# A feed-forward stage in which 9 of 22 gate/up pairs are computed as seven block products for eight, and the down product in two parts

## The chip, the cores and the metric

One core of a Trainium2 chip (trn2), one launch. The metric is device time in microseconds (us), the median of three runs. Engines are named as in the profile: PE is TensorE's matmuls, PEld its weight loads, DVE is VectorE, ACT is ScalarE, POOL is GpSimd, SP is the engine that issues the weight transfers.

## The reference, cut to what matters

x holds 512 tokens of 1024 channels. Two blocks of one kind and one of another run one after the other; each has a token mixer (not touched here), and together they have four feed-forward stages of this form, with 2816 = 22 x 128 inner channels:

```
h = rms_norm(x, w_norm)
g = h @ w_gate            # 1024 -> 2816
u = h @ w_up              # 1024 -> 2816
x = x + s * ((silu(g) * u) @ w_down)   # 2816 -> 1024, s is 1.0 or 0.5
```

All of it is float32. After the last stage comes a final rms_norm.

## The kernel before, in words

**Layout.** Channels lie on the 128 partitions and tokens along the free dimension, so x is 8 tiles of 128x512. A product is made of rows: one 128x128 block of weights times one 128x512 tile. Each operand is split into a rounded high part and the rest (WHI, WLO for the weights; HHI, HLO for h; FHI, FLO for the inner activations), and a row is three matmuls, lines 1469 to 1471: high x high, high x rest of the tile, rest of the weights x high. One output tile of gate or up is 8 rows (24 matmuls of 512 columns).

**A feed-forward stage** (`ffn`, line 505). For each j of 22: the gate product, then on DVE `gs` (line 2278: PSUM times the root of the norm), on ACT `silu` (line 1873), the up product, on DVE `mul` (line 2285), on ACT `fhi` (line 1877, the high part), on DVE `flo` (line 2289, the rest). Then the down product: 8 output tiles of 22 rows each, and for each tile `add` on DVE (lines 2299 and 2301). The norm's scale is applied after the product, which is why h itself is only x times a weight. The last tile of the last stage is computed in two halves of 256 tokens (`last_tile`, line 531; matmuls on lines 1558 to 1560), and each half goes through `hadd` (lines 2313, 2314), the final norm's sums and root, and eight `hscale` (line 2324) before it is stored. `last_half` (line 553) emits hadd, hsq, hsum, hroot and the eight hscale of a half.

**Weights.** They come as one stream of slots, each up to 8 rows (512 KB). SP loads slot k into one of four raw buffers (`load`, line 2730; it waits for the split of slot k - 4). ACT casts the high part (`high`, line 1805), DVE subtracts it (`low`, line 2216). Four split buffers: `high` of slot k waits until PE has finished slot k - 4.

**The order of work.** `Order` (line 209) simulates the whole kernel and emits one list of steps; every engine runs its steps in that list's order, and waits on semaphores. PE's steps advance the planner's clock `now`; a step of another engine gets an end time from that engine's own backlog and the table `TIMES`, and the planner does not make it wait for steps it depends on. A *chain* (a generator) sleeps until a time or until the end time of a step, and is resumed at the next `beat`, which comes after each PE row. `advance` (line 270) emits `high` for slots up to three past the last one taken and less than four past the last one released; `split` emits the slot's `low` once `high` has its end time. These few lines set how the splits are ordered:

```
while self.next_split < min(self.next_slot + look, self.used + SPL, len(self.slots)):
    self.spawn(self.split(k, self.add("high", k)))
...
for engine, us in TIMES.get(step[0], ()):
    t = self.engine_end[engine] = max(t, self.engine_end[engine]) + us
```

Entries of TIMES used below (us): row 0.68, high 1.0031, low 1.23, gs 1.005, silu 1.4753, mul 0.64242, fhi 1.0912, flo 0.21674; HANDOVER, added to each end time, is 0.17528. The change adds srow 0.36, snap 0.4, dd 0.45, ww 1.0, cc 0.95, tsum 3.0, thi 1.03, tlo 1.23, padd 2.5532. They are the planner's figures, not measurements.

## Time and profile before

| | us |
|---|---|
| median of 3 runs | 2700.85 (2699.92 to 2701.69) |
| span of the profiled execution | 2697.8 |
| PE busy in it | 2665.9 (99%) |
| PEld busy | 2195.1 (81%) |
| DVE busy | 1526.9 (57%) |
| ACT busy | 1173.5 (43%) |

The span runs from the first to the last instruction of one execution. Its own device time was not listed apart from the runs; the median lies 3.05 us above the span. A matmul's duration in the trace includes its way through the array, so consecutive matmuls overlap, and what a stream costs is read from the distance of their starts. "idle before <- X" names what ended an engine's wait.

### The profile page before, as it was taken

How to read it: one execution, taken by the hardware profiler on the slowest of the kernel's cores; microseconds unless marked ns; L12 is line 12 of the kernel's file. 1: busy time of each engine (PE TensorE's matmuls, PEld its weight loads, DVE VectorE, ACT ScalarE, POOL GpSimd, SP SyncE). 2: the span in 40 equal slices, each digit the busy share in tenths (PEclk: the TensorE clock that was granted, in tenths of full speed). 3: DMA queues.
4: the chain of work that ended last, by engine and by line, in shares of the span. 5: the costliest groups of instructions: out<-in, count | busy, mean ns of one | idle time of the engine just before them, and what ended most of it. 6: DMA issues, size and time to landing. Idle time of an engine off the chain costs nothing.

```text
span 2697.8 us, 33846 instructions
## 1 busy us (share of the span) xinstructions
PE 2665.9 (99%) x13860; PEld 2195.1 (81%) x13860; DVE 1526.9 (57%) x2142; ACT 1173.5 (43%) x1732; POOL 26.8 (1%) x45
## 2 busy tenths in 40 slices
PE   9989999999989999999999999999999999999998
PEld 8777888888777888888888888888777888888887
DVE  7885444345885444344444356899978844544433
ACT  6784332225784322233322234455688452432221
POOL 0000000000000000000000000000000000000000
PEclk9999999999999999999999999999999999999999
DMA  6303333324303333333333342222223432333332
GB/s 216 94 2 110 100 96 95 98 83 148 94 2 110 102 94 97 97 94 97 100 94 96 98 138 86 72 74 76 77 86 96 133 94 94 98 98 94 98 94 67
DMA packets 75801, 255.55 MB, mean 95 GB/s; under 512 B 9088, under 2 KB 12288, under 8 KB 75264
## 3 DMA queue, kind: packets, MB, share of 16 engines
q1 hardware_dynamic: 73136, 240.29, 29.3%
q0 software_dynamic: 2512, 13.11, 1.3%
q8 instruction: 110, 1.80, 0.3%
q14 instruction: 43, 0.35, 0.0%
HBM read 241.30 MB, written 8.39 MB: 93 GB/s over the span
## 4 chain that ended last, share of the span: by engine, by line
PE 93%; DVE 4%; ACT 3%; issue 1%; DVEq 0%; ACTq 0%
PE PS L1469 27%; PE PS L1471 27%; PE PS L1470 27%; PE PS L1719 1%; PE PS L1701 1%; PE PS L1428 1%; PE PS L1488 1%; PE PS L1487 1%; PE PS L1489 1%; DVE WLO L2216 0%; PE PS L1665 0%; ACT WHI L1805 0%; PE PS L1537 0%; PE PS L1535 0%; PE PS L1539 0%
## 5 line engine op out<-in xcount | busy, mean ns | idle before, releaser
L1469 PE MATMUL PS<-HHI,WHI 128*128 128x512 f32 x2256 | 893.2, 396 | 0.0
L1471 PE MATMUL PS<-HHI,WLO 128*128 128x512 f32 x2256 | 878.8, 390 | 0.0
L1470 PE MATMUL PS<-HLO,WHI 128*128 128x512 f32 x2256 | 878.3, 389 | 0.0
L2216 DVE TENSOR_TENSOR WLO<-WR,WHI 128x1024 fp32r<-128x1024 f32 (+2 forms) x450 | 535.0, 1191 | 495.4 <-ACT WHI L1805 492.2
L1805 ACT CAST WHI<-WR 128x1024 fp32r<-128x1024 f32 (+2 forms) x450 | 457.5, 1018 | 445.6 <-PE PS L1471 421.9
L1469 PEld LDWEIGHTS PS<-HHI,WHI 128*128 128x128 f32 x2256 | 423.6, 188 | 92.1 <-issue 4.8
L1470 PEld LDWEIGHTS PS<-HLO,WHI 128*128 128x128 f32 x2256 | 423.7, 188 | 89.9 <-issue 4.1
L1471 PEld LDWEIGHTS PS<-HHI,WLO 128*128 128x128 f32 x2256 | 423.4, 188 | 88.8
L1469 PE MATMUL PS<-FHI,WHI 128*128 128x512 f32 x682 | 265.3, 389 | 0.0
L1470 PE MATMUL PS<-FLO,WHI 128*128 128x512 f32 x682 | 265.3, 389 | 0.0
L1471 PE MATMUL PS<-FHI,WLO 128*128 128x512 f32 x682 | 265.3, 389 | 0.0
L1877 ACT CAST FHI<-SQF 128x512 fp32r<-128x512 f32 x88 | 54.5, 620 | 330.3 <-DVE SQF L2285 330.3
L1873 ACT ACTIVATE SQF<-SQF 128x512 f32<-128x512 f32 x88 | 55.6, 632 | 307.4 <-DVE SQF L2278 307.3
L2606 DVE SCALAR_TENSOR_TENSOR CVA<-CU,VEC,CVA 128x511 f32<-128x511 f32 (+14 forms) x240 | 162.9, 730 | 1.8 <-ACT CVA L2110 1.8
L2285 DVE TENSOR_TENSOR SQF<-SQF,PS 128x512 f32<-128x512 f32 x88 | 60.6, 688 | 166.0 <-PE PS L1471 162.1
L1469 PEld LDWEIGHTS PS<-FHI,WHI 128*128 128x128 f32 x682 | 128.0, 188 | 26.8
L1470 PEld LDWEIGHTS PS<-FLO,WHI 128*128 128x128 f32 x682 | 128.0, 188 | 26.5
L1471 PEld LDWEIGHTS PS<-FHI,WLO 128*128 128x128 f32 x682 | 128.0, 188 | 26.4
L2278 DVE TENSOR_TENSOR SQF<-PS,RS 128x512 f32<-128x512 f32 x88 | 60.8, 691 | 142.2 <-PE PS L1471 140.9
L1469 PE MATMUL PS<-YHI,WHI 128*128 128x512 f32 x320 | 128.1, 400 | 2.2 <-DVE WLO L2216 2.1
L1471 PE MATMUL PS<-YHI,WLO 128*128 128x512 f32 x320 | 124.7, 390 | 0.0
L1470 PE MATMUL PS<-YLO,WHI 128*128 128x512 f32 x320 | 124.6, 389 | 0.0
(381 smaller groups left out, 2727.5 us busy)
## 6 DMA issues: line engine op xcount, KB each, us to landing
WR<-in_stream SPq DMA_DIRECT2D x402, 512.0 KB, 3.6
WR<-in_stream SPq DMA_DIRECT2D x32, 384.0 KB, 3.0
xkeep<-X POOLq DMA_DIRECT2D x3, 2048.0 KB, 9.4
X<-xkeep POOLq DMA_DIRECT2D x24, 256.0 KB, 4.7
WR<-in_stream SPq DMA_DIRECT2D x16, 328.0 KB, 4.0
ROT<-RQ SPq DMA_DIRECT2D x40, 64.0 KB, 2.0
X<-in_xin SPq DMA_DIRECT2D x8, 256.0 KB, 4.9
out<-X SPq DMA_DIRECT2D x8, 256.0 KB, 2.2
```

Source lines behind the costliest of these rows:

```text
L1428: t = e.transpose(out[:, i * P:(i + 1) * P], src, ident)
L1469: e.matmul(out, hi[:, i, :], xhi, start=first, stop=False)
L1470: e.matmul(out, hi[:, i, :], xlo, start=False, stop=False)
L1471: t = e.matmul(out, lo[:, i, :], xhi, start=False, stop=final)
L1487: e.matmul(out, xhi, hi[:, i, :], start=r == 0, stop=False)
L1805: e.copy(hi, raw).then_inc(S["act_high"], 1)
L1873: e.activation(SQ[:, j % 2, :], SQ[:, j % 2, :], ACT.Silu).then_inc(S["act_silu"], 1)
L1877: e.copy(FHI[:, j, :], HF[:, j % 2, :]).then_inc(S["act_xhigh"], 1)
L2216: e.tensor_tensor(lo, raw, hi.bitcast(F32), ALU.subtract).then_inc(S["dve_low"], 1)
L2278: e.tensor_tensor(SQ[:, j % 2, :], PS[o.bank["gate", f, j]][:, :], RS[:, :], ALU.mult).then_inc(S["dve_gs"], 1)
L2285: e.tensor_tensor(HF[:, j % 2, :], SQ[:, j % 2, :], PS[o.bank["up", f, j]][:, :], ALU.mult).then_inc(S["dve_mul"], 1)
L2606: e.scalar_tensor_tensor(acc[:, s:T], CU[:, j, 0:T - s], vec("cvw", 8 * (TAPS - 1 - s) + j), acc[:, s:T], ALU.mult, ALU.add).then_inc(S["d ...
```

## The change

Of the 22 gate/up pairs of each stage, the nine with j = 5, 7, ..., 21 (`SEVEN`) are computed in another way. The block matrix [gate, up] (two halves of 512 input channels each) times the two halves of 256 tokens is a 2x2 by 2x2 block product, and it is formed by seven products (Strassen's scheme in Winograd's form) in place of eight. One product is 4 rows of three matmuls with 256 columns. At the start of a stage `combined` makes four sums of the tokens' blocks (`sv`, `ss`, `sd`, split by `sshi`, `sslo`). For each such pair `weight_sums` makes four sums of the weight blocks on DVE (`tsum`, four adds of 512 columns from the two raw slots), splits them (`thi` on ACT and `tlo` on DVE, two of 1024 columns each), and during and after the products DVE and ACT put the outputs together (`snap`, `dd`, `ww`, a `gs` in two halves, `cc`). The up slot's own split covers half of its columns. The sums' buffers also serve for the outputs, so `tsum` of pair j waits for `mul` of pair j - 2.

The down product is in two parts of 11 rows (`PARTS`): after pair 10 all eight output tiles get their first 11 rows and are added to x (`padd`), after pair 21 the other 11. FHI and FLO shrink to 11 tiles each. A down tile's weights come in slots of 6 and 5 rows. In a stage the planner gives six PSUM banks to the products and two to the rest, before four and four.

The diff, cut; `eight` is the loop body of before:

```diff
...
 SPL = 4
 LOOK = 3
 SLOT = 1024
+PARTS = (range(0, 11), range(11, 22))
+PART = 11
+DOWN = (((0, 6), (6, 5)), ((11, 6), (17, 5)))
+SEVEN = range(5, FT, 2)
+PRODUCTS = ((0, 0, True), (1, 0, True), (2, 0, True), (0, 1, False), (0, 0, False), (1, 0, False), (2, 0, False))
 HALVES = (slice(0, T // 2), slice(T // 2, T))
 LEVELS = (1, 2, 4, 8, 16, 32, 64)
...
             fm("w_in", l, c * P)
         for j in range(DT):
             fm("w_out", l, j * P)
-        for j in range(FT):
-            fm("w_gate", l, j * P)
-            fm("w_up", l, j * P)
-        for j in range(DT):
-            fm("w_down", l, j * P, down)
+        for part, down in zip(PARTS, DOWN):
+            for j in part:
+                fm("w_gate", l, j * P)
+                fm("w_up", l, j * P)
+            for j in range(DT):
+                fm("w_down", l, j * P, down)
 
...
     def advance(self, look=LOOK):
         while self.next_split < min(self.next_slot + look, self.used + SPL, len(self.slots)):
             k = self.next_split
+            if k - RAW in self.pair_of and not self.summed(self.pair_of[k - RAW]):
+                break
             self.next_split += 1
             self.spawn(self.split(k, self.add("high", k)))
...
+        for pair in SEVEN:
+            at_ = self.slots.index((gate, i, 0, DT, pair * P, P))
+            self.pair_of[at_] = self.pair_of[at_ + 1] = (f, pair)
...
+        self.ring.update(main=(0, 1, 2, 3, 4, 5), side=(6, 7))
+        self.spawn(self.combined(f))
+        for part, rows in zip(PARTS, DOWN):
+            for j in part:
+                if j + 1 in SEVEN:
+                    self.spawn(self.weight_sums(f, j + 1))
+                if j in SEVEN:
+                    self.seven(f, gate, up, i, up0, j)
+                else:
+                    self.eight(f, gate, up, i, up0, j)
+                self.add("fhi", f, j)
+                self.add("flo", f, j)
...
+            if part is PARTS[-1]:
+                self.ring.update(main=(0, 1, 2, 3), side=(4, 5, 6, 7))
+            for j in range(DT):
+                if part is not PARTS[-1]:
+                    self.product(("part", f, j), ("F", f), down, i, j * P, rows)
+                    self.x["padd", f, j] = self.x_now[j]
+                    self.x_now[j] = self.add("padd", f, j)
+                    self.free(("part", f, j), ("dve_add", self.x_now[j]))
+                elif (f, j) == (len(NORM_FFN) - 1, DT - 1):
+                    self.last_tile(f, down, i, j)
+                else:
+                    self.product(("out", ADD_FFN[f], j), ("F", f), down, i, j * P, rows)
+                    self.add_to_x(ADD_FFN[f], AFTER_NORM[m], j)
...
+    def seven(self, f, gate, up, i, up0, j):
+
+        keys = ("seven", f, j, 0), ("seven", f, j, 1), ("seven", f, j, 2)
+        for key in keys:
+            self.take(key)
+        slots = self.slot(gate, i, 0, j * P), self.slot(up, i, 0, up0 + j * P)
+        self.slot_of["seven", f, j] = slots
+        self.run(lambda: ("tlo", f, j, 1) in self.n)
+        for u in range(7):
+            for r in range(4):
+                self.add("srow", f, j, u, r)
+                if r == 3:
+                    if u in (4, 6):
+                        self.release()
+                    else:
+                        self.products += 1
+                        self.product_end[f, j, u] = self.products
+                self.beat()
+            if u == 0 or u == 2:
+                self.add("snap", f, j, u // 2)
+            elif u == 1:
+                self.add("dd", f, j)
+            elif u == 5:
+                self.add("ww", f, j)
+                self.free(keys[0], ("dve_gs", self.add("gs", f, j)))
+                self.add("silu", f, j)
+        self.free(keys[1], ("dve_gs", ("gs", f, j)))
+        self.free(keys[2], ("dve_gs", self.add("cc", f, j)))
...
+
+        yield from self.added(("sslo", f, 3))
+        last = max(k for k, pair in self.pair_of.items() if pair == (f, j))
+        while last - RAW not in self.low:
+            yield 0.1
+        yield self.add("tsum", f, j)
+        self.advance()
+        for k in range(2):
+            self.add("thi", f, j, k)
+        for k in range(2):
+            yield ("thi", f, j, k)
+            self.add("tlo", f, j, k)
 
     def last_tile(self, f, down, i, j):
 
...
+            return hi[:, 4:8, :], lo[:, 4:8, :]
+        i = {1: 1, 2: 0, 3: 3, 5: 2}[u]
+        return (x[:, i, :].rearrange("p (r c) -> p r c", r=4) for x in (THI, TLO))
+
+    def block_tokens(u, r):
+
+        if u in (0, 4):
+            return HHI[:, u + r, HALVES[0]], HLO[:, u + r, HALVES[0]]
+        if u == 3:
+            return HHI[:, 4 + r, HALVES[1]], HLO[:, 4 + r, HALVES[1]]
+        i = {1: 1, 2: 0, 5: 3, 6: 2}[u]
+        return SHI[:, i, r, :], SLO[:, i, r, :]
+
     def totals(j, h):
 
         if h == 1:
...
                     t.then_inc(S["pe_slot"], 1)
+            elif kind == "srow":
+                f, j, u, r = a
+                bank, half, fresh = PRODUCTS[u]
+                k_gate, k_up = o.slot_of["seven", f, j]
...
+                    if fresh:
+                        emptied(q, ("seven", f, j, bank))
+                    if u == 0:
+                        weights_split(q, k_gate)
+                        q.wait_ge(S["dve_ulo"], n["ulo", NORM_FFN[f], DT - 1])
+                    elif u == 1:
+                        q.wait_ge(S["dve_xlow"], n["tlo", f, j, 1])
+                        q.wait_ge(S["dve_xlow"], n["sslo", f, 3])
+                    elif u == 3:
+                        q.wait_ge(S["act_uhi"], n["snap", f, j, 0])
+                    elif u == 5:
+                        q.wait_ge(S["dve_gs"], n["dd", f, j])
+                    elif u == 6:
+                        weights_split(q, k_up)
+                        q.wait_ge(S["act_uhi"], n["snap", f, j, 1])
+                hi, lo = block_weights(f, j, u)
...
                     q.wait_ge(S["pe_slot"], k - SPL + 1)
+                if k in o.pair_of and k - 1 in o.pair_of:
+                    hi, raw = hi[:, T:2 * T], raw[:, T:2 * T]
...
+                if k == 3:
+                    for r in range(4):
+                        t = e.activation(SUMS[3][:, r, :], SV[:, r, :], ACT.Copy, scale=norm_weight(NORM_FFN[f], r))
+                    settle(t)
+                e.copy(SHI[:, k, :, :].rearrange("p r t -> p (r t)"), combination(f, k)).then_inc(S["act_xhigh"], 1)
+            elif kind == "thi":
+                f, j, k = a
+                q.wait_ge(S["dve_scale"], n["tsum", f, j])
+                if j - 2 in SEVEN:
+                    q.wait_ge(S["pe_slot"], o.slot_of["seven", f, j - 2][1] + 1)
+                e.copy(THI[:, 2 * k:2 * k + 2, :].rearrange("p u c -> p (u c)"), WT[k][:, :, :].rearrange("p u c -> p (u c)")
+                       ).then_inc(S["act_xhigh"], 1)
+            elif kind == "snap":
+                f, j, k = a
+                q.wait_ge(S["dve_xlow"], n["tlo", f, j, 1])
+                q.wait_ge(S["pe_prod"], o.product_end[f, j, 2 * k])
+                e.copy((P1, Q5)[k], PS[o.bank["seven", f, j, 2 * k]][:, HALVES[0]]).then_inc(S["act_uhi"], 1)
             elif kind == "uhi":
                 m, j = a
                 x_ready(q, o.x[step])
...
+            elif kind == "tsum":
+                f, j = a
+                k_gate, k_up = o.slot_of["seven", f, j]
+                (gate, _, _), (up, _, _) = slot_tiles(k_gate), slot_tiles(k_up)
+                for k in (k_gate, k_up):
+                    q.wait_ge(s_w[k % RAW], 16 * (k // RAW + 1))
+                if j - 2 in SEVEN:
+                    q.wait_ge(S["dve_mul"], n["mul", f, j - 2])
+                else:
+                    q.wait_ge(S["dve_xlow"], n["sslo", f, 3])
+                settle(e.tensor_tensor(WT[0][:, 0, :], gate[:, 0:T], up[:, 0:T], ALU.add))
+                e.tensor_tensor(WT[1][:, 0, :], up[:, 0:T], up[:, T:2 * T], ALU.add)
+                settle(e.tensor_tensor(WT[0][:, 1, :], WT[0][:, 0, :], up[:, T:2 * T], ALU.add))
+                e.tensor_tensor(WT[1][:, 1, :], WT[0][:, 1, :], gate[:, T:2 * T], ALU.add).then_inc(S["dve_scale"], 1)
...
+            elif kind == "dd":
+                f, j = a
+                q.wait_ge(S["act_uhi"], n["snap", f, j, 0])
+                q.wait_ge(S["pe_prod"], o.product_end[f, j, 1])
+                e.tensor_tensor(DD, PS[o.bank["seven", f, j, 1]][:, HALVES[0]], P1, ALU.subtract).then_inc(S["dve_gs"], 1)
+            elif kind == "ww":
+                f, j = a
+                q.wait_ge(S["pe_prod"], o.product_end[f, j, 5])
+                settle(e.tensor_tensor(WW, PS[o.bank["seven", f, j, 1]][:, HALVES[0]], P1, ALU.subtract))
+                if j >= 2:
+                    q.wait_ge(S["dve_mul"], n["mul", f, j - 2])
+                e.tensor_tensor(SQ[:, j % 2, HALVES[1]], PS[o.bank["seven", f, j, 0]][:, HALVES[1]], WW, ALU.subtract
+                                ).then_inc(S["dve_gs"], 1)
+            elif kind == "gs" and a[1] in SEVEN:
+                f, j = a
+                rooted(q, NORM_FFN[f])
+                q.wait_ge(S["pe_slot"], o.slot_of["seven", f, j][0] + 1)
+                e.tensor_tensor(SQ[:, j % 2, HALVES[0]], PS[o.bank["seven", f, j, 0]][:, HALVES[0]], RS[:, HALVES[0]], ALU.mult)
+                q.wait_ge(S["dve_gs"], n["ww", f, j])
+                e.tensor_tensor(SQ[:, j % 2, HALVES[1]], SQ[:, j % 2, HALVES[1]], RS[:, HALVES[1]], ALU.mult).then_inc(S["dve_gs"], 1)
+            elif kind == "cc":
+                f, j = a
+                q.wait_ge(S["act_uhi"], n["snap", f, j, 1])
+                q.wait_ge(S["dve_gs"], n["gs", f, j])
+                e.tensor_tensor(UP2[:, HALVES[1]], WW, Q5, ALU.add)
+                q.wait_ge(S["pe_slot"], o.slot_of["seven", f, j][1] + 1)
+                e.tensor_tensor(UP2[:, HALVES[0]], PS[o.bank["seven", f, j, 2]][:, HALVES[0]], DD, ALU.add).then_inc(S["dve_gs"], 1)
+            elif kind == "mul" and a[1] in SEVEN:
+                f, j = a
+                q.wait_ge(S["act_silu"], n["silu", f, j])
+                q.wait_ge(S["dve_gs"], n["cc", f, j])
+                q.wait_ge(S["act_xhigh"], n["fhi", f, j - 2])
+                e.tensor_tensor(HF[:, j % 2, :], SQ[:, j % 2, :], UP2, ALU.mult).then_inc(S["dve_mul"], 1)
+            elif kind == "padd":
+                f, j = a
+                done(q, ("part", f, j))
+                x_ready(q, o.x[step])
+                rooted(q, NORM_FFN[f])
+                q.wait_ge(S["dve_add"], n[step] - 1)
+                settle(e.tensor_tensor(HF[:, 0, :], PS[o.bank["part", f, j]][:, :], RS[:, :], ALU.mult))
+                e.scalar_tensor_tensor(X[:, j, :], HF[:, 0, :], ADD_SCALE[ADD_FFN[f]], X[:, j, :], ALU.mult, ALU.add
+                                       ).then_inc(S["dve_add"], 1)
...
                     q.wait_ge(S["dve_low"], n[o.low[k - RAW]])
+                    if k - RAW in o.pair_of:
+                        q.wait_ge(S["dve_scale"], n[("tsum", *o.pair_of[k - RAW])])
...
```

## Rows read from the trace of the kernel before

**Rows 1.** The page, parts 1 and 2: span, busy time and the granted clock
```profile
span 2697.8 us, 33846 instructions
...
PE 2665.9 (99%) x13860; PEld 2195.1 (81%) x13860; DVE 1526.9 (57%) x2142; ACT 1173.5 (43%) x1732; POOL 26.8 (1%) x45
...
PEclk9999999999999999999999999999999999999999
```

**Rows 2.** Windows in the last feed-forward stage: pairs, down product, halved tile
```profile
core 0: us, PE busy (x) PEld busy (x) DVE busy (x) ACT busy (x) POOL busy (x), PEclk, DMA share, GB/s
2352.00:2560.00 208.00, 208.00 (x919) 172.26 (x918) 87.05 (x96) 59.77 (x76) 0.00 (x0) 1.00 0.32 96
...
2572.00:2671.00 99.00, 99.00 (x438) 81.97 (x438) 34.42 (x37) 22.64 (x26) 0.00 (x0) 1.00 0.26 82
2671.00:2688.00 17.00, 17.00 (x137) 16.72 (x136) 5.39 (x12) 3.23 (x5) 0.00 (x0) 1.00 0.04 13
```

**Rows 3.** Timeline, DVE over one pair: start, duration, engine, line, tiles
```profile
2414.80 0.69 DVE L2285 TENSOR_TENSOR SQF<-SQF,PS 128x512 f32<-128x512 f32 x1 [1.95 <-PE PS L1471]
2416.17 0.69 DVE L2289 TENSOR_TENSOR FLO<-SQF,FHI 128x512 fp32r<-128x512 f32 x1 [0.69 <-ACT FHI L1877]
2417.13 1.23 DVE L2216 TENSOR_TENSOR WLO<-WR,WHI 128x1024 fp32r<-128x1024 f32 x1 [0.26 <-ACT WHI L1805]
2420.17 0.69 DVE L2278 TENSOR_TENSOR SQF<-PS,RS 128x512 f32<-128x512 f32 x1 [1.82 <-PE PS L1471]
2425.68 0.69 DVE L2285 TENSOR_TENSOR SQF<-SQF,PS 128x512 f32<-128x512 f32 x1 [1.95 <-PE PS L1471]
```

**Rows 4.** Timeline, ACT over the same pair
```profile
2415.52 0.62 ACT L1877 CAST FHI<-SQF 128x512 fp32r<-128x512 f32 x1 [3.93 <-DVE SQF L2285]
2416.05 1.05 ACT L1805 CAST WHI<-WR 128x1024 fp32r<-128x1024 f32 x1
2420.89 0.63 ACT L1873 ACTIVATE SQF<-SQF 128x512 f32<-128x512 f32 x1 [3.80 <-DVE SQF L2278]
2421.43 1.04 ACT L1805 CAST WHI<-WR 128x1024 fp32r<-128x1024 f32 x1
```

**Rows 5.** Timeline, PE: last 512-column, first and two later 256-column matmuls
```profile
2671.34 0.39 PE L1471 MATMUL PS<-FHI,WLO 128*128 128x512 f32 x1
2671.57 0.28 PE L1558 MATMUL PS<-FHI,WHI 128*128 128x256 f32 x1
...
2679.98 0.28 PE L1558 MATMUL PS<-FHI,WHI 128*128 128x256 f32 x1
...
2683.58 0.28 PE L1558 MATMUL PS<-FHI,WHI 128*128 128x256 f32 x1
```

**Rows 6.** Timeline, DVE, the last tile and the end
```profile
2671.77 0.69 DVE L2299 TENSOR_TENSOR SQF<-PS,RS 128x512 f32<-128x512 f32 x1 [2.20 <-PE PS L1471]
...
2680.54 0.42 DVE L2313 TENSOR_TENSOR SQF<-PS,RS 128x256 f32<-128x256 f32 x1 [5.96 <-PE PS L1560]
2681.00 0.43 DVE L2314 SCALAR_TENSOR_TENSOR X<-SQF,X 128x256 f32<-128x256 f32 x1
2685.54 3.26 DVE L2324 SCALAR_TENSOR_TENSOR X<-X,VEC,SQF 128x256 f32<-128x256 f32 x8 [4.11 <-ACT SQF L1788]
2688.88 0.42 DVE L2313 TENSOR_TENSOR SQF<-PS,RS 128x256 f32<-128x256 f32 x1
```

**Rows 7.** Timeline, a weight split that PE waited for (out-projection of block one)
```profile
230.20 3.50 DVE L2216 TENSOR_TENSOR WLO<-WR,WHI 128x1024 fp32r<-128x1024 f32 x3 [12.62 <-ACT WHI L1805]
...
230.68 0.39 PE L1471 MATMUL PS<-YHI,WLO 128*128 128x512 f32 x1
...
231.48 0.50 PE L1469 MATMUL PS<-YHI,WHI 128*128 128x512 f32 x1 [0.41 <-DVE WLO L2216]
...
231.82 0.40 PE L1470 MATMUL PS<-YLO,WHI 128*128 128x512 f32 x1
```

**Rows 8.** The page, part 6: the weight transfers, KB each, median us to landing
```profile
WR<-in_stream SPq DMA_DIRECT2D x402, 512.0 KB, 3.6
```

More of the change, by code:

```diff
@@ L43 @@
     **dict.fromkeys(["xT", "bT", "zT", "pT"], "turn"),
-    **dict.fromkeys(["add", "hadd"], "add"),
+    **dict.fromkeys(["add", "hadd", "padd"], "add"),
+    **dict.fromkeys(["uhi", "snap"], "uhi"),
+    **dict.fromkeys(["gs", "dd", "ww", "cc"], "gs"),
+    **dict.fromkeys(["scale", "ss", "sd", "tsum"], "scale"),
     **dict.fromkeys(["xscale", "hscale"], "xscale"),
@@ L65, in tm @@
             s.append((name, i, r0, 2, c0, 512))
-    down = ((0, 8), (8, 8), (16, 6))
     for l in range(2):
@@ L353, in product @@
         self.rhs[p] = rhs
+        self.first[p] = rows[0][0]
         self.take(p)
@@ L510, in ffn @@
         self.run()
-        for j in range(FT):
-            if j > 0:
-                self.product(("gate", f, j), ("U", m), gate, i, j * P)
-            self.free(("gate", f, j), ("dve_gs", self.add("gs", f, j)))
-            self.add("silu", f, j)
-            if j > 0:
-                self.product(("up", f, j), ("U", m), up, i, up0 + j * P)
-            self.free(("up", f, j), ("dve_mul", self.add("mul", f, j)))
-            self.add("fhi", f, j)
-            self.add("flo", f, j)
-            if m == 5 and 4 <= j < 4 + DT:
-                self.x["xscale", 4, j - 4] = self.x_now[j - 4]
-                self.x_now[j - 4] = self.add("xscale", 4, j - 4)
@@ L524, in ffn @@
-        for j in range(DT):
-            if (f, j) == (len(NORM_FFN) - 1, DT - 1):
-                self.last_tile(f, down, i, j)
-                continue
-            self.product(("out", ADD_FFN[f], j), ("F", f), down, i, j * P, ((0, 8), (8, 8), (16, 6)))
-            self.add_to_x(ADD_FFN[f], AFTER_NORM[m], j)
+        self.ring.update(main=(0, 1, 2, 3, 4, 5), side=(6, 7))
+        self.spawn(self.combined(f))
+        for part, rows in zip(PARTS, DOWN):
+            for j in part:
+                if j + 1 in SEVEN:
[6 more added lines that the diff above has]
+                self.add("flo", f, j)
+                if m == 5 and 5 <= j < 5 + DT // 2:
+                    self.run(lambda: ("sd", f) in self.n)
+                    for t in (2 * j - 10, 2 * j - 9):
+                        self.x["xscale", 4, t] = self.x_now[t]
+                        self.x_now[t] = self.add("xscale", 4, t)
+            if part is PARTS[-1]:
+                self.ring.update(main=(0, 1, 2, 3), side=(4, 5, 6, 7))
+            for j in range(DT):
+                if part is not PARTS[-1]:
[8 more added lines that the diff above has]
+                    self.add_to_x(ADD_FFN[f], AFTER_NORM[m], j)
@@ new lines, in eight @@
+    def eight(self, f, gate, up, i, up0, j):
+        m = NORM_FFN[f]
+        if j > 0:
+            self.product(("gate", f, j), ("U", m), gate, i, j * P)
+        self.free(("gate", f, j), ("dve_gs", self.add("gs", f, j)))
+        self.add("silu", f, j)
+        if j > 0:
+            self.product(("up", f, j), ("U", m), up, i, up0 + j * P)
+        self.free(("up", f, j), ("dve_mul", self.add("mul", f, j)))
+    def seven(self, f, gate, up, i, up0, j):
[22 more added lines that the diff above has]
+                self.free(keys[0], ("dve_gs", self.add("gs", f, j)))
+                self.add("silu", f, j)
+        self.free(keys[1], ("dve_gs", ("gs", f, j)))
+        self.free(keys[2], ("dve_gs", self.add("cc", f, j)))
+        self.add("mul", f, j)
@@ L544, in last_tile @@
         self.spawn(self.last_half(0))
-        for r in range(FT):
+        for r in PARTS[-1]:
             _, i, nr = self.slot_of[p, r]
@@ L1411, in x_ready @@
         kind, i, *j = made if made[0] != "xload" else (made[0], 0, made[1])
-        if kind == "xload":
+        if kind == "padd":
+            q.wait_ge(S["dve_add"], n[made])
+        elif kind == "xload":
             q.wait_ge(s_x[j[0]], 16)
@@ L1473, in tensor_engine @@
                     t.then_inc(S["pe_slot"], 1)
+            elif kind == "srow":
+                f, j, u, r = a
+                bank, half, fresh = PRODUCTS[u]
+                k_gate, k_up = o.slot_of["seven", f, j]
+                out = PS[o.bank["seven", f, j, bank]][:, HALVES[half]]
+                if r == 0:
+                    if fresh:
[14 more added lines that the diff above has]
+                hi, lo = block_weights(f, j, u)
+                xhi, xlo = block_tokens(u, r)
+                kw = {"skip_group_check": True}
+                e.matmul(out, hi[:, r, :], xhi, start=fresh and r == 0, stop=False, **kw)
+                e.matmul(out, hi[:, r, :], xlo, start=False, stop=False, **kw)
+                t = e.matmul(out, lo[:, r, :], xhi, start=False, stop=r == 3, **kw)
+                if r == 3:
+                    t.then_inc(S["pe_slot" if u in (4, 6) else "pe_prod"], 1)
             elif kind == "trow":
```

128 lines of the change are left out of this document (105 added, 23 removed).

## The prediction

> **What bounds the kernel now.** I read the page first, then windows by stage, then the timeline of one pair engine by engine. On the page PE is busy for 99% of the span and its granted clock stands at the upper level, 2.4 GHz, in every slice [rows 1]; in the windows of a feed-forward stage PE is busy for all of each window, at pairs, down product and halved tile alike, with DVE at 42% and ACT at 29% in the pairs [rows 2]. So PE's stream sets the time, and DVE's and ACT's work costs nothing as long as it arrives in time. What a stream costs is the distance of starts. Two `mul` lie 10.88 us apart [rows 3], 48 matmuls of 512 columns, 0.2267 each. From 2679.98 to 2683.58 there are 30 steps of 256 columns, 0.1200 each [rows 5], at the same clock [rows 2].
>
> **What it removes on PE.** A pair of seven products is 84 matmuls of 256 columns, 84 x 0.1200 = 10.08, for 10.88: 0.80 less. Nine pairs, four stages: 36 x 0.80 = **-28.8 us**. Both widths carry 0.0133 above their columns at 2.4 GHz (0.2133 and 0.1067), and with 1.75 times the matmuls this eats 36 x 36 x 0.0133 = 17 us of the ideal gain of 46. The down product keeps its rows, 8 x 22, so its PE time is unchanged.
> The Trainium skill (TensorE: Matmul & The Clock Gate, Back-to-back issue gap) has a gap of N/2.4 + 2.5 ns, 215.8 and 109.2 ns for these widths; by it a pair would fall from 10.36 to 9.17 us and the gain would be 43 us. The rows differ from it, and the sum goes by them.
>
> **The end: +4.0.** In the last tile the second half's rows run on PE while the first half is normalised. Its `hadd` starts at 2688.88, just behind the eight `hscale` of the first half (2685.54 + 3.26 = 2688.80) [rows 6]. The list order stays (the planner emits the first half's eight `hscale` at its last row of half two, before the second `hadd`), so all behind the first half keeps its times, but PE has 11 rows to do there instead of 22: 11 x 3 x 0.1200 = 4.0 us of PE work moves ahead of it and is no longer hidden.
>
> **Smaller parts, at nothing.** `padd` is 2 x 0.69 on DVE per down tile, which lasts 7.5 us; two slots of 6 and 5 rows cost one split more per 15 us; the cover is DVE's idle half. Without it a down tile would wait for a bank, and there are six. The token sums are 12 operations of 256 columns, one of 1024 and four splits of 1.23: about 11 us of DVE and 7.5 of ACT, over pairs 1 to 4 (43 us), where DVE's own work is 2 x 1.23 + 3 x 0.69 = 4.5 us a pair [rows 3]. `tsum` of pair 11 waits on DVE for a transfer (3.6 us to landing [rows 8]) in the down product's sixth tile; the next split in its queue is wanted 10 us later. In pairs SP's load of slot k waits for `tsum` too; it has some 10 us in hand.
>
> **The sums of the weights: the term that decides.** A block-product pair (call its start 0) is followed by an ordinary one (10.08) and the next block-product pair (20.96), whose second product needs the second `tlo` at 22.40. `tsum` needs the buffers that `mul` of the pair before frees. I follow the planner's list through one such period. At the end of the fifth product (7.20) the gate slot is released and `high`, `low` of the next gate are emitted; the planner has `low` due at 8.38 and emits it at the beat of 8.64, ahead of `ww`. After pair and `mul`, `flo`, it emits `tsum` at the first beat of the ordinary pair, to end at 16.86. That is after 15.52, where `gs`, `silu` of the ordinary pair and `high` of the next slot are emitted. So the orders are: DVE low, ww, gs, cc, mul, flo, tsum, low, gs, low, tlo, tlo; ACT high, silu, fhi, high, silu, high, thi, thi.
> Durations: 256 columns 0.42 [rows 6]; 512 columns 0.69, 1024 columns 1.23 [rows 3]; ACT 0.62 and 1.04 [rows 4]. An operation behind an independent one starts 0.09 before that one's end [rows 4, 7], behind a dependent one on its engine 0.04 after [rows 6], behind another engine 0.03 after [rows 3, 4], behind PE's boundary 0.20 after [rows 5, 6]. (ACT's wait there I take as 0.25.)
> - high 7.45 to 8.49, low to 9.75; ww 9.66 to 10.54, gs to 11.20, cc 11.24 to 11.99 (PE ended the pair at 10.08, so DVE is late by then);
> - mul to 12.72, fhi to 13.37, flo 13.40 to 14.09, tsum (four adds, two settled) to 16.75, half low to 17.35, gs to 17.95;
> - silu to 18.61, high 18.52 to 19.56, low 19.59 to 20.82 (DVE idle 1.6 us behind that cast), tlo to 21.96, tlo to 23.10.
> Wanted at 22.40: 0.70 late. PE resumes with a loss: in the trace a split ended at 230.20 + 1.23 = 231.43, and the second matmul started at 231.82, 0.39 later for 0.23 [rows 7], so +0.16: **0.86 us a pair**. Everything here hangs on PE's clock of the pair, so the wait comes again each period and doesn't fade. It concerns pairs 7, 9, 13, 15, 17, 19, 21, which have such a pair two before: 28 in all, 28 x 0.86 = **+24.1 us**. In the third stage two `xscale` follow `flo` of pairs 5 and 7 (2 x 0.60 = 1.2 each time, a 512-column operation at 0.69 less the overlap): **+2.4**.
> Below, the wait could be 0.45 (twenty operations, 0.02 less each), above 1.4 (0.03 more each, for the semaphore waits that no row of before shows between halves): 13 to 39 us. I take 0.86, as every duration in it has a row. Steps added behind the late `tlo`: `mul` to 23.7, fhi to 24.35, high to 25.3, `snap` (a 256-column copy, taken as 0.42) to 25.65; PE wants it before the fourth product, at 23.26 + 2.88 = 26.15. It holds by 0.5.
> **Sum:** -28.8 + 4.0 + 24.1 + 2.4 = +1.7. Other stages are replanned from a slightly other state: +-3, at 0. The span would be 2699.5, and with the 3.05 between span and median 2702.6. I allow one more microsecond for a first wait where a stage's DVE queue is late, and say **2704**.
>
> **Rivals.**
> 1. *The sums arrive in time.* For it: DVE work per period is about 16 of 20.96 us, and 0.70 is 3% of the chain; if the true list puts `thi` ahead of `silu` and `high` of the ordinary pair, the cast's 1.04 and the idle 1.6 go. Against: the order follows from the table with 1.3 us to spare. Then -28.8 + 4.0 and up to 2.4: 2676 to 2679. Chance 0.25.
> 2. *A second wait behind the first* (the other side). `snap` of the first product has 0.5 us in hand on ACT, and `mul`, `fhi` and a cast must pass first, all behind the late `tlo`. If these four handovers take 0.5 us more than reckoned, PE stops again ahead of the fourth product, and everything behind the fifth product moves with it. From there each further 0.5 to 1.0 a pair is 14 to 28 us: 2718 to 2732. For it: the queue is in order on both engines. Against: every handover of before takes 0.03 [rows 3, 4]. Chance 0.12.
> 3. *The 256-column stream is not 0.1200 in this place.* It was measured on 66 rows of one kind. At 0.124: 36 x 84 x 0.004 = +12, 2716; chance 0.05. With a fixed part of 2.5 ns rather than 13.3 both widths would be faster, the gain 43 and the end 2690; the trace shows neither width at it, chance 0.01. The Trainium skill's gap (the same section) is that case; the trace disagrees with 13.3.
> 4. The change does what it says on PE (84 matmuls for 48 stand in the code), so that rival has no chance of its own.
>
> **How the numbers follow.** The forecast case has 0.57: 0.86 within 0.45 to 1.4, and +-3 elsewhere, gives 2688 to 2721. The range takes in rival 1 down to 2676 and the foot of rival 2 up to 2724, and leaves out some 0.12. A measurement of this kernel tells about 0.2% from no change, 5.4 us: 2695.4 to 2706.3. Of the forecast case 0.15 falls below that, 0.48 inside, 0.37 above. Faster: 0.25 + 0.01 + 0.09 = 0.35. Same: 0.27. Slower: 0.21 + 0.12 + 0.05 = 0.38. The forecast's middle lies in "same", but no case of size does.
>
> **What would show it.** Right: 256-column matmuls 0.1200 apart in the new lines; in the list of waits, PE waiting for the DVE split of the weight sums 28 times, 0.7 to 0.9 us each, and in no other place of these stages; DVE's `low` ahead of `ww`; PE's busy share under 99%; the first half's `hscale` still ending 8.5 us after that half. Wrong: no such wait (rival 1), a wait of PE for ACT's copy of the first product (rival 2), other spacing (rival 3), or idle PE at the starts of stages or in the down products, which I costed at nothing.

## The result and the profile after

The changed kernel takes **2716.78 us** (median of 4 runs, 2715.88 to 2718.63), the kernel before beside it 2700.39 (4 runs): ratio 1.0062, 95% interval 1.0048 to 1.0077. That is 16 us slower. The forecast was 2704 in a range of 2676 to 2724, so the sign it leaned to and the range held, and the size was 13 us short. The profiled execution has a span of 2714.1 us, against 2697.8 [rows 1].

A line of the page of the changed kernel, part 1:

```profile
PE 2647.5 (98%) x15123; PEld 2235.5 (82%) x15123; DVE 1823.8 (67%) x2738; ACT 1380.4 (51%) x2028; POOL 26.7 (1%) x45
```

PE is down from 99% to 98%, with 84 matmuls of 256 columns in place of 48 of 512 in each of 36 pairs. The list of waits of PE in the changed kernel (us in total, times, longest):

```profile
PE PS L1634 <- DVE TLO L2459: 30.0, 29, 5.8
PE PS L1733 <- ACT SQF L2054: 5.2, 1, 5.2
```

The first line is new: PE waits for the split of the weight sums (`tlo`), 29 times. The second, PE's last sum behind the second half's square, stood before too, at 1.4 us. In the timeline of PE in the changed kernel (two regular waits, one period apart):

```profile
478.33 0.28 PE L1636 MATMUL PS<-HHI,WLO 128*128 128x256 f32 x1
479.42 0.35 PE L1634 MATMUL PS<-SHI,THI 128*128 128x256 f32 x1 [0.82 <-DVE TLO L2459]
479.62 0.28 PE L1635 MATMUL PS<-SLO,THI 128*128 128x256 f32 x1
...
479.85 0.28 PE L1634 MATMUL PS<-SHI,THI 128*128 128x256 f32 x1
...
480.20 0.28 PE L1634 MATMUL PS<-SHI,THI 128*128 128x256 f32 x1
...
501.43 0.36 PE L1634 MATMUL PS<-SHI,THI 128*128 128x256 f32 x1 [0.81 <-DVE TLO L2459]
```

Once it runs, the stream goes at 0.36 per three, as [rows 5] have it. The two waits are 22.01 us apart, where the prediction's period is 20.96: 1.05 is lost. By the starts: the matmul was due at 478.45 and started at 479.42, 0.97 late, and the next came 0.20 behind it instead of 0.12. (The 0.82 shown as idle begins at the modelled end of the matmul before, 0.28 behind its start.)

The timeline of DVE in the changed kernel, from the `flo` of one block-product pair to the late `tlo` (x2 is both halves):

```profile
491.60 0.69 DVE L2576 TENSOR_TENSOR FLO<-SQF,FHI 128x512 fp32r<-128x512 f32 x1 [0.69 <-ACT FHI L2075]
492.21 0.68 DVE L2452 TENSOR_TENSOR WT<-WR 128x512 f32<-128x512 f32 x1
...
495.46 0.68 DVE L2565 TENSOR_TENSOR SQF<-PS,RS 128x512 f32<-128x512 f32 x1
497.79 1.23 DVE L2416 TENSOR_TENSOR WLO<-WR,WHI 128x1024 fp32r<-128x1024 f32 x1 [1.64 <-ACT WHI L1972]
498.93 2.35 DVE L2459 TENSOR_TENSOR TLO<-WT,THI 128x1024 fp32r<-128x1024 f32 x2
```

This is the order of the prediction, with the idle 1.64 us behind the cast of the next slot (1.6 there). The period's zero, reckoned back from its sixth product (start 485.24, less 7.20), is 478.04, so the second `tlo` ends at 501.28 = 23.24, where the prediction had 23.10 and PE wants it at 22.40.

**One wait is unlike the others.** The timeline of PE and then windows of the changed kernel, pair 5 of the third stage (columns of windows: length; busy us and instructions of PE, PEld, DVE, ACT, POOL; granted clock):

```profile
1278.24 0.28 PE L1636 MATMUL PS<-HHI,WLO 128*128 128x256 f32 x1
1284.32 0.55 PE L1634 MATMUL PS<-SHI,THI 128*128 128x256 f32 x1 [5.80 <-DVE TLO L2459]
...
1285.10 0.41 PE L1634 MATMUL PS<-SHI,THI 128*128 128x256 f32 x1
1285.32 0.41 PE L1635 MATMUL PS<-SLO,THI 128*128 128x256 f32 x1
```

```profile
1280.00:1290.00 10.00, 5.68 (x37) 5.71 (x38) 6.34 (x7) 6.03 (x8) 0.00 (x0) 0.66 0.47 168
1290.00:1300.00 10.00, 10.00 (x63) 9.01 (x62) 6.30 (x12) 4.11 (x5) 0.00 (x0) 1.00 0.03 12
```

PE stood 5.8 us, and when it went on, the granted clock was at the lower level for some 3 us: starts 0.215 apart instead of 0.120 (1285.10, 1285.32), about 1.4 us more. The timeline of DVE there in the changed kernel says why the sums are late: the last split of the token sums ends only at 1274.96, just ahead of `tsum` and 2.0 us ahead of pair 5's start on PE (1276.93). In the first stage it ends 9.3 us ahead of it (299.55 for 308.87).

```profile
1273.74 1.22 DVE L2440 TENSOR_TENSOR SLO<-SUM,SHI 128x1024 fp32r<-128x1024 f32 x1
1275.10 0.69 DVE L2452 TENSOR_TENSOR WT<-WR 128x512 f32<-128x512 f32 x1
...
1281.82 2.35 DVE L2459 TENSOR_TENSOR TLO<-WT,THI 128x1024 fp32r<-128x1024 f32 x2
```

**Where the 16.3 us of span come from** (starts in the two traces, a stage being from its first `gs` to the last addition into X): stages 1, 2 and 4 come out even, within 0.2 us (for stage 4 its end is taken apart), so their 7.2 us of gain each are paid back by their waits; stage 3 is longer by 9.8; the end by 3.85; the stretch between stages 1 and 2 by 1.2 and that between 3 and 4 by 1.7. That is 16.5, and the small rests take 0.2 off.

The last two can be read in the traces. The 1.2 is one wait of PE that the kernel before has not, in the mixer between the first and second stages (0.9 idle, the rest in the restart):

```profile
PE PS L1605 <- ACT Z L2083: 0.9, 1, 0.9
```

The 1.7 is the granted clock. In the mixer between the third and fourth stages PE stops for 1.89 us in both kernels. The timeline of PE at the stop and the window behind it, first of the kernel before, then of the changed one:

```profile
2060.46 1.98 PE L1766 MATMUL PS<-XB,GW 128*128 128x512 f32 x4 [1.89 <-DVE XB L2613]
2062.00:2066.00 4.00, 4.00 (x19) 3.11 (x18) 3.85 (x6) 3.97 (x5) 0.00 (x0) 1.00 0.49 136
```

```profile
2071.34 2.88 PE L1931 MATMUL PS<-XB,GW 128*128 128x512 f32 x4 [1.89 <-DVE XB L2900]
2072.00:2076.00 4.00, 4.00 (x10) 2.30 (x9) 3.93 (x6) 3.96 (x5) 0.00 (x0) 0.57 0.42 133
```

Behind the same stop the clock stayed up in one execution and fell in the other. That mixer is not touched by the change, and changed kernels without the fall exist too (e5_order2, e11_best7 below), so this 1.7 us is no steady part of the change.

### The profile page after: what moved, and what is told of

Its sections match the earlier page's. It is cut to its first block, busy times and chain, and to the rows that moved or that the text cites. A ratio compares the mean times of both kernels' runs of the same rounds, so it can differ in the third digit from the quotient of the medians.

```text
span 2714.1 us, 37462 instructions
## 1 busy us (share of the span) xinstructions
PE 2647.5 (98%) x15123; PEld 2235.5 (82%) x15123; DVE 1823.8 (67%) x2738; ACT 1380.4 (51%) x2028; POOL 26.7 (1%) x45
## 4 chain that ended last, share of the span: by engine, by line
PE 74%; DVE 17%; ACT 6%; issue 3%; DVEq 0%; ACTq 0%
PE PS L1605 18%; PE PS L1606 18%; PE PS L1607 18%; DVE WLO L2416 4%; PE PS L1634 3%; PE PS L1636 3%; PE PS L1635 3%; ACT WHI L1972 3%; DVE TLO L2459 2%; PE PS L1884 1%; PE PS L1866 1%; PE PS L1564 1%; DVE WT L2453 1%; DVE WT L2452 1%; DVE SQF L2565 1%
## 5 line engine op out<-in xcount | busy, mean ns | idle before, releaser
L2416 DVE TENSOR_TENSOR WLO<-WR,WHI 128x1024 fp32r<-128x1024 f32 (+4 forms) x482 | 518.9, 1081 | 450.3 <-ACT WHI L1972 447.9
L1972 ACT CAST WHI<-WR 128x1024 fp32r<-128x1024 f32 (+4 forms) x482 | 448.3, 931 | 514.1 <-PE PS L1607 410.7
L1605 PE MATMUL PS<-HHI,WHI 128*128 128x512 f32 x1680 | 670.5, 399 | 0.9 <-ACT Z L2083 0.9
L1607 PE MATMUL PS<-HHI,WLO 128*128 128x512 f32 x1680 | 654.9, 390 | 0.0
L1606 PE MATMUL PS<-HLO,WHI 128*128 128x512 f32 x1680 | 654.9, 390 | 0.0
L1605 PEld LDWEIGHTS PS<-HHI,WHI 128*128 128x128 f32 x1680 | 315.8, 188 | 70.6 <-issue 5.0
L1607 PEld LDWEIGHTS PS<-HHI,WLO 128*128 128x128 f32 x1680 | 315.5, 188 | 67.0
L1606 PEld LDWEIGHTS PS<-HLO,WHI 128*128 128x128 f32 x1680 | 316.0, 188 | 66.2 <-issue 4.4
L1634 PE MATMUL PS<-SHI,THI 128*128 128x256 f32 x432 | 125.0, 289 | 30.0 <-DVE TLO L2459 30.0
L1635 PE MATMUL PS<-SLO,THI 128*128 128x256 f32 x432 | 122.7, 284 | 0.0
```

The source lines that it names most:

```text
L1605: e.matmul(out, hi[:, i, :], xhi, start=first, stop=False)
L1606: e.matmul(out, hi[:, i, :], xlo, start=False, stop=False)
L1607: t = e.matmul(out, lo[:, i, :], xhi, start=False, stop=final)
L1634: e.matmul(out, hi[:, r, :], xhi, start=fresh and r == 0, stop=False, **kw)
L1635: e.matmul(out, hi[:, r, :], xlo, start=False, stop=False, **kw)
L1972: e.copy(hi, raw).then_inc(S["act_high"], 1)
```

## The experiments

Each is an edit of the changed kernel. The runs of before beside them had medians of 2699.91 (e1 to e4), 2700.67 (e5 to e8) and 2700.65 us (e9 to e11).

**e1_parts: the change without its block products**

```
-SEVEN = range(5, FT, 2)
+SEVEN = range(0)
-        self.spawn(self.combined(f))
-                    self.run(lambda: ("sd", f) in self.n)
```

> All 22 pairs of a stage as eight products again; the down product stays in two parts, with its smaller slots, padd and six banks. Theory A (the tail): the parts cost only what is no longer hidden at the end, +4.0 us, so 2704 to 2705; PE waits nowhere in the four stages; the first half's hscale end about 9 us after that half, as in the changed kernel. Rival B (the parts themselves stall PE: banks, slots of 6 and 5 rows, padd): well above 2706, with PE's waits inside the down products. Rival C (the parts are free): 2700.4.

2705.39 us, ratio 1.0020 (1.0011 to 1.0029), +5.5 us. The split `tlo` is gone from the waits, the four stages take their old time (within 0.01 us, the end apart), and PE waits in none of their down products: rival B did not occur. So the two-part down product alone costs 5.5. Its trace has 3.85 at the end and 1.2 in the wait for `Z` of above, so theory A missed that wait. The profiled execution took 2707.48 us, 2.1 more than the median, and has two stretches of lower clock, at the mixer's stop of above (1.7 us) and near 186 us (about 1.1). What the 36 block-product pairs add to that is 16.4 - 5.5 = 10.9 us: they lose by themselves.

**e2_order: the weight sums' splits straight behind the sums, in both queues**

```
-        yield self.add("tsum", f, j)
+        self.add("tsum", f, j)
```

> All of the change, but the planner emits the casts of the weight sums (thi) at once behind tsum instead of at tsum's planned end, so that on ACT they stand ahead of silu and the next slot's cast, and on DVE both tlo stand ahead of gs and the next low. PE's list is the same, the work is the same. Theory A (the order of the lists makes the wait): the second tlo is ready some 2 us early, the 27 regular waits of PE (1.06 us each with the restart, 2.4 in the third stage) go, and pair 5 of the third stage waits about 3 us less: 2716.8 less 31 less 3, 2682 to 2687, faster than both kernels. Rival B (DVE as a whole is too full, 67% busy and more in the stages): the wait moves to another place, mul, snap or a weight split, and the time stays above 2700.

2717.26 us, ratio 1.0065 (1.005 to 1.008): nothing gained, against theory A. The wait moved. The waits of this kernel:

```profile
PE PS L1634 <- ACT WT L2001: 25.7, 26, 2.2
...
PE PS L1634 <- DVE TLO L2459: 3.6, 1, 3.6
```

Its timeline, DVE, PE and ACT in turn:

```profile
496.66 2.36 DVE L2459 TENSOR_TENSOR TLO<-WT,THI 128x1024 fp32r<-128x1024 f32 x2 [0.52 <-ACT THI L1995]
498.94 0.68 DVE L2565 TENSOR_TENSOR SQF<-PS,RS 128x512 f32<-128x512 f32 x1
501.25 1.23 DVE L2416 TENSOR_TENSOR WLO<-WR,WHI 128x1024 fp32r<-128x1024 f32 x1 [1.64 <-ACT WHI L1972]
```

```profile
505.00 0.39 PE L1634 MATMUL PS<-HHI,THI 128*128 128x256 f32 x1 [0.92 <-ACT WT L2001]
```

```profile
503.11 0.62 ACT L2075 CAST FHI<-SQF 128x512 fp32r<-128x512 f32 x1 [1.89 <-DVE SQF L2572]
...
504.59 0.36 ACT L2001 COPY WT<-PS 128x256 f32<-128x256 f32 x1
```

`tlo` is early now, but the ordinary pair's `gs` stands behind both of them, and with it `silu`, the cast of the next slot, that slot's split, `mul`, `fhi`, one more cast and only then ACT's copy of the first product. PE stands ahead of the fourth product: the place that the prediction's rival 2 named, at 0.92. The idle 1.64 on DVE is still there, behind `gs` instead of ahead of `tlo`. Both steps are wanted by PE. That the chain through both is too long as long as it holds that idle time is an argument here; the next run tests it.

**e5_order2: `gs` first, then the sums' splits, the cast of the next slot last**

```
         self.free(("gate", f, j), ("dve_gs", self.add("gs", f, j)))
+        ahead = ("tsum", f, j + 1) in self.n and ("thi", f, j + 1, 0) not in self.n
+        if ahead:
+            self.add("thi", f, j + 1, 0)
         self.add("silu", f, j)
+        if ahead:
+            self.add("thi", f, j + 1, 1)
+            self.add("tlo", f, j + 1, 0)
+            self.add("tlo", f, j + 1, 1)
...
-        yield self.add("tsum", f, j)
+        self.add("tsum", f, j)
+        if ("gs", f, j - 1) not in self.n:
+            return
+        yield ("tsum", f, j)
```

> All of the change; in the ordinary pair ahead of a block-product pair the steps are emitted as gs, thi, silu, thi, tlo, tlo, and only then the next slot's cast and low (in the run before, thi stood ahead of gs and silu, and the wait moved to the copy of the first product). Work and PE's list as in the changed kernel. Theory A (the order of two in-order lists makes the wait, not their load): second tlo at 20.8 and the copy of the first product at 24.7, for 22.4 and 25.3 wanted, so no regular wait in stages 1, 2 and 4, at most 0.6 twice in stage 3, and pair 5 of stage 3 waits 2 to 3 us less: 2683 to 2688. Rival B (the two engines can't carry it in any order): a third place waits, about 1 us a pair, and the time stays at 2710 or more.

**2682.76 us**, ratio 0.9939 (0.9922 to 0.9956), 34 us less than the change. Same operations, same data, another order in two queues: the order made the waits, not the load, and rival B is out. Its timeline of DVE and of PE:

```profile
490.56 0.68 DVE L2575 TENSOR_TENSOR SQF<-PS,RS 128x512 f32<-128x512 f32 x1
...
492.89 1.23 DVE L2469 TENSOR_TENSOR TLO<-WT,THI 128x1024 fp32r<-128x1024 f32 x1 [0.50 <-ACT THI L2005]
494.03 1.22 DVE L2426 TENSOR_TENSOR WLO<-WR,WHI 128x1024 fp32r<-128x1024 f32 x1
```

```profile
495.43 0.28 PE L1646 MATMUL PS<-HHI,WLO 128*128 128x256 f32 x1
495.55 0.28 PE L1644 MATMUL PS<-SHI,THI 128*128 128x256 f32 x1
```

The 1.64 us of waiting became work (0.50 is left), the second `tlo` ends at 494.12, and PE takes it at 495.55 with no gap: 1.4 us in hand. In its list of waits one for `tlo` is left, 3.5 us at pair 5 of the third stage (and 0.8 in two for the copy of the first product). In this trace 33 of the 36 block-product pairs take 10.07 us on PE and the period is 20.98, as the prediction had them without waits. At pair 5 of the third stage the wait fell from 5.8 to 3.5; the rest goes with the late token sums (e6_all below emits them early and has no wait there).

**e4_spaced: five of 22 pairs, four apart**

```
-SEVEN = range(5, FT, 2)
+SEVEN = range(5, FT, 4)
...
-                if j - 2 in SEVEN:
+                if j - 4 in SEVEN:
```

> Block products only for pairs 5, 9, 13, 17, 21 (20 of 36 in all), so that no such pair has one two before it and tsum does not wait for a mul that has just been late. Theory A: 20 x 0.80 = -16.0 for PE's stream, the tail +4, the late pair 5 of the third stage +7.5, no regular waits: 2700.4 - 4.5 = 2696, up to 2699 with what the stages between give. Rival B (block products are dear on PE in themselves, spacing or restarts): each pair removed from the changed kernel makes it faster by the same amount, 2716.8 - 16 x 0.45 = 2709.

2698.20 us, ratio 0.9992 (0.9983 to 1.0002). One wait for `tlo` is left, again the 5.8 us at pair 5. In the traces stages 1 and 2 are 3.9 us shorter than before with five such pairs each, 0.78 a pair for the forecast's 0.80: a pair does take about 10.08 us where its sums come in time, and rival B is out. The sum with 20 pairs at 0.80 less, 5.5 for the parts and 7.2 for pair 5 is -3.3, measured -1.7.

**e10_from7: block products from pair 7 on**

```
-SEVEN = range(5, FT, 2)
+SEVEN = range(7, FT, 2)
```

> The changed kernel, with block products from pair 7 on instead of pair 5 (8 pairs a stage, 32 in all). Theory A (pair 5 of the third stage costs its own wait of 5.8 us and 1.4 us of half clock, and pair 7, whose predecessor pair but one is then ordinary, loses its wait too): +3.2 for four block-product pairs less, -7.2, -2.4 (third stage) and -3 x 1.06 for pair 7: -9.6 us, 2706 to 2709. Rival B (the late token sums of the third stage then hold up pair 7 by as much, since DVE's queue is behind for the whole stage): +3.2 - 4 x 1.06, about 2715 to 2717.

2705.46 us, ratio 1.0020 (1.001 to 1.0029); the span fell by 9.8 us (2714.1 to 2704.3), the theory's 9.6, and the median is 0.5 below its range. The third stage alone is 8.8 us shorter. The waits for `tlo` are 24, longest 2.1, so the 5.8 us and pair 7's waits are gone. A window of this kernel where PE had stood:

```profile
1280.00:1290.00 10.00, 10.00 (x45) 8.29 (x45) 5.70 (x7) 3.77 (x6) 0.00 (x0) 1.00 0.30 101
```

No idle time and no lower clock: four gains given up, and the kernel is 11 us faster than the change.

**e3_name: the step `dd` under another name**

```
-    "dd": (("dve", 0.45),)
+    "df": (("dve", 0.45),)
```

The name `dd` also stands in the program's list of steps that need ACT's table of logarithm and exponential, so each block-product pair loads two tables, as the timeline of ACT in the changed kernel has it:

```profile
481.76 1.28 ACT L1963 ACT_TABLE_LOAD   x1
...
485.49 1.05 ACT L1972 CAST WHI<-WR 128x1024 fp32r<-128x1024 f32 x1 [2.06 <-PE PS L1636]
486.56 1.28 ACT L2069 ACT_TABLE_LOAD   x1
489.29 0.63 ACT L2069 ACTIVATE SQF<-SQF 128x512 f32<-128x512 f32 x1 [1.45 <-DVE SQF L2481]
```

> Only the step dd is renamed to df, so that it no longer stands in the table of functions: 72 table loads of 1.28 us on ACT go (two in each block-product pair), nothing else is different. Theory A (they lie in ACT's idle time: the first before the copy of the third product, the second before a silu that waits for gs): 2716 to 2717, no difference. Rival B (they delay silu and with it mul and the sums of the weights): up to 36 x 0.5 = 18 us faster, about 2700.

2717.32 us, ratio 1.0063 (1.0048 to 1.0078): no difference. 72 loads of 1.28 us, 92 us of ACT, lie in time in which ACT waited anyway (1.45 and 2.06 above).

**e8_tail: the first half's eight `hscale` behind the second `hadd`**

```
         self.add("hroot", h)
+        if h == 0:
+            yield from self.added(("hadd", 1))
```

> The changed kernel, only the second half's hadd is emitted ahead of the first half's eight hscale. Theory A (the tail's loss is DVE's queue: the second hadd stands behind 3.3 us of hscale while PE has long been done): PE's last sum no longer waits 5.2 us, the end is 2.5 to 3.5 us earlier, 2713 to 2714.5. Rival (it only swaps which half is late): no difference, 2716 to 2717.

2713.68 us, ratio 1.0049 (1.0034 to 1.0064): 3.1 us less than the change, and PE's last sum waits 1.4 us for 5.2. In the changed kernel the eight `hscale` keep the second `hadd` waiting, in this one `hadd` goes first. First the changed kernel's end, then this one's:

```profile
2701.50 3.26 DVE L2611 SCALAR_TENSOR_TENSOR X<-X,VEC,SQF 128x256 f32<-128x256 f32 x8 [4.96 <-ACT SQF L1953]
2704.67 0.42 DVE L2600 TENSOR_TENSOR SQF<-PS,RS 128x256 f32<-128x256 f32 x1
...
2708.26 3.26 DVE L2611 SCALAR_TENSOR_TENSOR X<-X,VEC,SQF 128x256 f32<-128x256 f32 x8 [2.72 <-ACT SQF L1953]
```

```profile
2703.76 0.42 DVE L2602 TENSOR_TENSOR SQF<-PS,RS 128x256 f32<-128x256 f32 x1 [4.36 <-PE PS L1727]
2704.22 0.43 DVE L2603 SCALAR_TENSOR_TENSOR X<-SQF,X 128x256 f32<-128x256 f32 x1
2704.57 6.42 DVE L2613 SCALAR_TENSOR_TENSOR X<-X,VEC,SQF 128x256 f32<-128x256 f32 x16
```

**e6_all and e9_best: everything together, with and without early token sums.** e6_all is e5_order2, e3_name and e8_tail with the token sums emitted ahead of pair 0, meant for the late sums of the third stage; e9_best is the same without that edit:

```
         self.spawn(self.mean_square(m))
+        self.spawn(self.combined(f))
         self.product_group(("U", m), [(("gate", f, 0), gate, i, 0), (("up", f, 0), up, i, up0)])
         self.run()
         self.ring.update(main=(0, 1, 2, 3, 4, 5), side=(6, 7))
-        self.spawn(self.combined(f))
```

> The run with the new order (gs, thi, silu, thi, tlo, tlo) and three more edits: the four sums of the tokens are emitted during the first pair, ahead of the norm's root; the step dd is renamed, so that 72 table loads on ACT go; the second half's hadd is emitted ahead of the first half's eight hscale. Theory A: pair 5 of stage 3 no longer waits and TensorE keeps its clock there (-4 to -7 against the new order alone), the end is 3 us shorter: 2674 to 2682. Rival (the early sums delay the root, and PE waits for a bank at the third pair): 2683 to 2690.

> The sums of the weights ahead of the up product, the renamed step, and the first half's hscale behind the second hadd; the token sums stay where the change has them (that is the kernel with everything together, less the early token sums). Theory A (early token sums were what made that kernel 15 us slower than the reordered one): 2682.8 less 3.1 for the tail, 2679 to 2681. Rival B (it was the renamed step or the tail together with the new order): 2692 to 2699 again. Rival C (the two gains overlap): 2682 to 2684.

e6_all: 2698.13 us, ratio 0.9991 (0.9982 to 1.0). e9_best: **2680.23**, ratio 0.9926 (0.991 to 0.9943). The early sums cost 18 us. They did remove the wait of pair 5, and put another at each stage's start (theory A of e9_best holds); PE's waits in e6_all, and one of them in its timeline:

```profile
PE PS L1617 <- DVE WLO L2428: 18.2, 8, 5.3
```

```profile
895.01 0.76 PE L1617 MATMUL PS<-HHI,WHI 128*128 128x512 f32 x1 [5.27 <-DVE WLO L2428]
```

Its timeline of DVE ahead of that:

```profile
888.80 1.23 DVE L2452 TENSOR_TENSOR SLO<-SUM,SHI 128x1024 fp32r<-128x1024 f32 x1 [2.86 <-ACT SHI L2001]
...
893.64 1.23 DVE L2428 TENSOR_TENSOR WLO<-WR,WHI 128x1024 fp32r<-128x1024 f32 x1 [0.25 <-ACT WHI L1984]
```

DVE stands 2.86 us for a cast of the token sums, with `gs`, `mul`, `flo` and the split that PE needs behind it in its queue. The waits at the four stages' starts are 5.27, 5.27, 4.82 and 0.68: 16.0 us, and the lower clock follows them too.

**e7_more: e6_all with pair 3 as well (ten of 22)**

> As the run with all four edits, with pair 3 as a tenth block-product pair of each stage. Theory A (a block-product pair gives 0.80 wherever its sums are ready): 4 x 0.80 = 3.2 us less than that run, if the early sums are ready for pair 3. Rival: they are not (sums of tokens 11 us of DVE, in a queue behind the root), PE waits 3 to 8 us at pair 3 of every stage, 10 to 30 us more.

2716.32 us, ratio 1.0059 (1.0044 to 1.0074), 18 us worse than e6_all, as the rival had it. Four waits for `tlo`, 13.3 us in all, come on top of the eight, and the mean granted clock falls to 0.991 (0.995 in e6_all): in this order the sums are not ready for pair 3.

**e11_best7: e9_best from pair 7 on**

> The kernel of e9_best with block products from pair 7 on. Theory A (only the third stage's wait of 3.5 us and its half clock of about 1 us go, four gains of 0.80 go too): -1.3 us against e9_best, 2678 to 2680. Rival B (pair 7 of the third stage waits instead): +2 to +3 against e9_best, 2681 to 2684.

**2676.82 us** (2676.51 to 2678.69), ratio **0.9915** (0.99 to 0.993), the fastest of all, 24 us below before and 40 below the change. Windows of the third stage, e9_best first and then e11_best7:

```profile
1265.00:1285.00 20.00, 17.33 (x104) 16.13 (x105) 13.75 (x21) 7.24 (x11) 0.00 (x0) 0.91 0.26 102
```

```profile
1265.00:1285.00 20.00, 20.00 (x90) 16.57 (x89) 14.07 (x18) 8.29 (x11) 0.00 (x0) 1.00 0.34 118
```

The medians fell by 3.4 where 1.3 was expected. In the traces pair 5 of the third stage had cost 5.2 us in e9_best (3.5 of wait, the rest restart and lower clock) and the wait at pair 7 another 0.8: 6.0 for the 4.5 that the theory took off, less 3.2 for the gains given up. The spans differ by 4.6, since e9_best's profiled execution also has 1.7 us of lower clock behind the mixer's stop, and this one has none.

## Why the prediction was right, and where it was short

The mechanism was right: less work on PE, a regular wait for the second `tlo`, and an end that is less hidden. The call itself owes something to luck: the range was 48 us wide, slower had 0.38 against 0.35 for faster, and 2704 itself lay in "same". Its step from span to median (3.05) is no constant: each execution here lies about 1.8 us above its own span (2715.88 for 2714.1).

- **PE's stream, -28.8: right.** Starts 0.120 apart in the new lines, and in e5_order2, where nearly all sums come in time, the pairs take 10.07 us for the forecast's 10.08. The Trainium skill's 109.2 ns for 256 columns (TensorE: Matmul & The Clock Gate, Back-to-back issue gap) is not met in this place either: 120 ns. That section gives the formula for an isolated matmul, not for a stream of weight loads and matmuls as here, which the prediction did not say.
- **The end, +4.0: right,** 3.85. e8_tail shows that the loss is a matter of list order, as the prediction had it, with 3.1 of it given back.
- **The wait for the second `tlo`: right in place, order and number, sized 0.2 short.** 28 forecast, 28 seen (the 29th in the list is pair 5 of the third stage); 21 of them at 0.81 to 0.87 us, 1.05 lost a pair for 0.86. The term was short in its handovers: 0.84 late for 0.70, then 0.15 to the start and 0.08 in the next matmul, where 0.16 was allowed. The last pair of each stage lost about 0.65. Stages 1, 2 and 4 lose 7.3, 7.0 and 7.1 us against 6.0 each, +3.4 in all.
- **Starts of stages, "at nothing": the step that failed.** The prediction spread the token sums over pairs 1 to 4 and compared totals with cover (11 us in 43). In stages 1, 2 and 4 that held: pair 5 has no wait. In the third the norm's root comes some 5.7 us later against PE (first `gs` to pair 5: 36.25 us for 41.98 in the first stage), DVE's queue lies behind it, and pair 5 needs its `tlo` by a fixed time: 5.8 us idle, 1.4 of lower clock. With the stage's longer waits at pairs 7 and 9 (2.14 each, as forecast with its two `xscale`) the stage lost 17.0 us where the prediction had 8.4, +8.6. e10_from7 shows that pair 5 is the cause: without it there the stage is 8.8 us shorter, one gain given up.
- **Other stages, +-3 at 0:** +2.8, the wait for `Z` (1.2) and a stretch of lower clock (1.7) that other executions don't have.
- **The sum with these terms:** 1.7 + 3.4 + 8.6 + 2.8 - 0.15 = 16.4, measured 16.3.
- **Rival 1** did not occur in the change, but e5_order2 makes it so: with the sums in time the rival's 2676 to 2679 was missed by 4 us, mostly the one wait left; with that gone too and the tail mended, e11_best7 is inside, with four gains fewer. The prediction's condition for it, `thi` ahead of `silu` and the cast, is not enough by itself: e2_order has it and gains nothing. **Rival 2** did not occur in the change: the copy ends at 481.74 and is wanted at 478.04 + 4.32 = 482.36, 0.6 in hand for the forecast's 0.5. In e2_order PE does stop at its place, but there the copy is late behind `gs` and `silu`, with `tlo` early. **Rival 3** is out: the spacing is 0.120.
- Left open: why the granted clock falls behind the mixer's stop in some executions only, and why PE waits for `Z` in the kernels with two parts. Giving the third stage alone another first pair was not tried.

## What to carry to other kernels

When a change gives a helper engine work with a due time inside the period of the engine that bounds, write out the in-order queues of one period, operation by operation, before counting busy shares: at 67% busy DVE was late each time, because a cast that nobody needed yet held it idle for 1.64 us ahead of the step that was needed. Mending one late step only moves the wait unless all steps wanted in that period fit, so reorder with the next one in view. Do the same sheet for the first period of each stage, where the queue begins late, and begin the scheme where its inputs can be ready: one pair a stage less was worth 11 us in the late order and 3 us in the good one.
